# Two padding tensors wider by 128 bytes: where the low weights and the hidden activations begin in SBUF

## The reference

```
first block, layer 0:  x = ffn(x); z = ffn(z); x = conv(x); z = conv(z); x = ffn(x); z = ffn(z)
first block, layer 1:  x = ffn(x); z = ffn(z); x = attention(x, keys of x and z); x = ffn(x)
second block, 2 layers: x = x + 0.5*ffn(x); x = x + mix(x) @ w_out; x = x + 0.5*ffn(x)

ffn(h)  = (silu(h @ w_gate) * (h @ w_up)) @ w_down        # 1024 -> 2 x 2816 -> 1024
conv(h) = (b * shortconv(c * u)) @ w_out, with b, c, u = split(h @ w_in)   # 1024 -> 3 x 1024 -> 1024
```

## Time and profile before

| | us |
|---|---|
| three timed runs | 2809.34, 2808.19, 2803.70 |
| their median | 2808.19 |
| the profiled execution, its own time | 2811.81 |
| its span, first to last instruction | 2809.8 |
| PE busy in it | 2734.7 (97%) |
| DVE, ACT, POOL busy | 1814.3, 1340.4, 799.1 |

### The profile page before, as it was taken

One profiled execution on the slowest core, in us unless ns is written; L12 is line 12 of the kernel. 1 busy time (PEld: TensorE's weight loads), 2 busy tenths in 40 slices (PEclk: granted clock), 3 DMA queues, 4 the chain that ended last, 5 costly groups with the idle time before them and its releaser, 6 DMA issues.

```text
span 2809.8 us, 59491 instructions
## 1 busy us (share of the span) xinstructions
PE 2734.7 (97%) x23696; PEld 2622.2 (93%) x23696; DVE 1814.3 (65%) x2505; ACT 1340.4 (48%) x1872; POOL 799.1 (28%) x768
## 2 busy tenths in 40 slices
PE   6999999999999999999998999999999999999999
PEld 4999999999999999999986998999889999987999
DVE  4655746777648567466466765765876566488664
ACT  3434434455435344344345444445764454377543
POOL 1322412124314224034001330321743223046330
PEclk9999999999999999999999999999999999999999
DMA  8765666566666656666621454555325555541554
GB/s 310 260 250 208 241 244 209 207 235 226 237 227 227 231 203 240 224 227 240 231 70 61 158 189 147 186 196 189 128 81 196 195 177 192 193 157 64 182 193 148
DMA packets 151711, 546.43 MB, mean 194 GB/s; under 512 B 16688, under 2 KB 20576, under 8 KB 151136
## 3 DMA queue, kind: packets, MB, share of 16 engines
q1 hardware_dynamic: 147632, 534.84, 55.4%
q10 hardware_dynamic: 3888, 8.86, 0.9%
HBM read 541.80 MB, written 1.84 MB: 193 GB/s over the span
## 4 chain that ended last, share of the span: by engine, by line
PE 90%; DVE 6%; ACT 2%; issue 1%; DMA 1%; ACTq 1%; SPq 0%; DVEq 0%
PE ps L414 28%; PE ps L415 27%; PE ps L416 27%; PE ps L441 2%; DVE w_lo L394 1%; DMA modraw<-wmod 1%; PE ps L825 1%; PE ps L809 1%; PE ps L798 1%; ACTq L1562 0%; DVE xT L1956 0%; DVE h_lo L1606 0%; ACT w_hi L386 0%; PE ps L893 0%; PE ps L700 0%
## 5 line engine op out<-in xcount | busy, mean ns | idle before, releaser
L394 DVE TENSOR_TENSOR w_lo<-raw,w_hi 128x1024 fp32r<-128x1024 f32 x874 | 1128.5, 1308 | 627.7 <-ACT w_hi L386 626.2
L414 PE MATMUL ps<-h_hi,w_hi 128*128 128x256 f32 (+1 forms) x4928 | 1384.7, 281 | 25.8 <-DVE h_lo L1606 13.2
L415 PE MATMUL ps<-h_lo,w_hi 128*128 128x256 f32 (+1 forms) x4928 | 1367.6, 278 | 0.0
L416 PE MATMUL ps<-h_hi,w_lo 128*128 128x256 f32 (+1 forms) x4928 | 1366.6, 277 | 0.0
L386 ACT ACTIVATE w_hi<-raw 128x1024 fp32r<-128x1024 f32 x874 | 894.2, 1053 | 507.3 <-PE ps L416 501.3
L414 PEld LDWEIGHTS ps<-h_hi,w_hi 128*128 128x128 f32 x4928 | 928.7, 188 | 47.2 <-issue 27.4
L415 PEld LDWEIGHTS ps<-h_lo,w_hi 128*128 128x128 f32 x4928 | 930.4, 189 | 0.8
L416 PEld LDWEIGHTS ps<-h_hi,w_lo 128*128 128x128 f32 x4928 | 930.2, 189 | 0.0
L2270 POOL CAST u_hi<-ut 128x256 fp32r<-128x256 f32 (+1 forms) x258 | 246.8, 957 | 1307.1 <-DVE ut L1764 747.6
L415 PE MATMUL ps<-u_lo,w_hi 128*128 128x256 f32 (+1 forms) x2064 | 581.1, 282 | 0.0
L414 PE MATMUL ps<-u_hi,w_hi 128*128 128x256 f32 (+1 forms) x2064 | 580.1, 281 | 0.2 <-DVE ut L1658 0.2
(11 more groups left out here) (317 smaller groups left out, 1743.9 us busy)
## 6 DMA issues: line engine op xcount, KB each, us to landing
raw<-wst SPq DMA_DIRECT2D x874, 512.0 KB, 3.7
modraw<-wmod SPq DMA_DIRECT2D x132, 512.0 KB, 5.6
headraw<-wmod SPq DMA_DIRECT2D x12, 512.0 KB, 10.0
mtab<-mixtabs ACTq DMA_DIRECT2D x2, 1673.5 KB, 7.7
xT<-xin ACTq DMA_DIRECT2D x2, 1024.0 KB, 23.8
atab<-attabs ACTq DMA_DIRECT2D x1, 1024.0 KB, 6.3
out<-xT SPq DMA_DIRECT2D x1, 1024.0 KB, 4.8
skew<-sqb ACTq DMA_DIRECT2D x1, 768.0 KB, 3.3
```

The lines of the kernel that those rows point to most:

```text
L394: dve.tensor_tensor(w_lo[:, s, :], raw[:, s, :], w_hi[:, s, :], ALU.subtract).then_inc(S("lo_ready"), 1)
L414: pe.matmul(psum, wh, hi, start=start, stop=False)
L415: pe.matmul(psum, wh, lo, start=False, stop=False)
L416: return pe.matmul(psum, wl, hi, start=False, stop=stop)
```

## The change

The unused tensor `before_w_lo` grows from 16 to 48 floats a partition, 128 bytes more. Every tensor allocated after it starts 128 bytes later; no instruction, wait or transfer is different, and the order on every engine is the same.

```
         raw = sb("raw", [P, RING, D])
-        sb("before_w_lo", [P, 16])
+        sb("before_w_lo", [P, 48])
         w_lo = sb("w_lo", [P, RING, D], F32R)
```

## The result

| | before | after |
|---|---|---|
| median of the runs, us | 2806.60 | 2823.60 |
| lowest to highest (4 runs each) | 2803.70 to 2809.34 | 2820.97 to 2827.61 |
| span of the profiled execution, us | 2809.8 | 2825.6 |

The fourth run of the kernel before, beside the three listed ahead, took 2805.01 us. The ratio is 1.0058, 95% interval 1.0043 to 1.0073: the change made the kernel slower by 17 us, where 26.6 us less were forecast. One correction to the title: only one padding tensor, `before_w_lo`, grew. u moved because it is allocated behind it.

What follows compares the result with a forecast made beforehand. PE's pace through its own matmuls was taken to bound the kernel; 27.7 us gained on u less 1.1 given back, all else 0, took the median 2808.2 to 2781.6, given as 2782 us, range 2772 to 2808.

Steps and rivals of the forecast that it cites:

- PE is the path: Whole kernel: PE busy for 97% of the span, dense matmuls stepping at a fast 113.3 or slow 118.9 ns.
- u from 96 to 224: Stages on u: 206 of 258 slow units (24 matmuls each) turn fast, 134 ns each, saving 27.7 us.
- w_lo from 160 to 32: Low-weight load beside matmuls on h: h already runs at the fast pace and keeps it, 0 us.
- The upper bound that I gave for one slot: Matmuls on h at line 415: should they turn slow in all 4576 tiles, 25.6 us lost.
- 1.1 us given back at the first cout stage: First cout stage: its 1.1 us gain may only lengthen PE's wait for h's second half, so taken off.
- 258 columns: Stage with 258 columns on h, at 120.8 ns: 7.0 us gained or lost possible, 0 taken.
- D: Rival: the 258-column stage turns fast as well, 7 us more saved, 2775 us; chance 12%.
- The other tensors: Moved attention, mixing layer and norm tensors: at most some 6 us either way, 0 taken.
- C: Rival: w_lo at 32 slows h, at line 415 (25.6 us, about 2807) or all three slots (76.9 us, 2859); 11%.
- A: Rival: the pace belongs to how a run begins, not to the address; no change, 2808 us; chance 10%.
- B: Rival: only part of u turns fast, as places may count modulo 512; some 13 us saved, about 2795; 13%.

Runs made afterwards that it cites:

- the map: Not the full kernel: matmuls alone on PE, 48 in a row, over places of w_hi and w_lo; with 258 columns the 64 pairs took 117.7 to 124.3 ns.

## Why the prediction was wrong

- *PE is the path, and a step of the dense matmuls is 113.3 or about 118 ns.* Right; PE's busy time and the span moved together.
- *u from 96 to 224: 206 slow units, 27.7 us.* The size was right for that move alone: 26.3 us on u, 25 in the time of the kernel with u alone. The reason was wrong. The forecast gave it to the place of u; what counts is u's distance to w_hi and to w_lo at once, which the move of u without w_lo sets to those of h before.
- *w_lo from 160 to 32: "I take 0 for h".* This is the step that failed. I judged each matmul by its own pair: h beside w_hi at (224, 32) ran fast in two slots of three, so the third would too with w_lo at 32. The runs show that the three slots are one pattern. With w_hi at 64 and w_lo at 192 behind the moving operand every start ends in the fast pace; with w_lo at 64, where w_hi is, both paces hold and what ran before decides. It cost 24.2 us on h and left u mixed (13.4 us gained instead of 26.3). The upper bound that I gave for one slot, 25.6 us, is close to the cost by luck: it is all three slots, in about half of the stretches, each step slower by 4.5 ns and not 5.6.
- *1.1 us given back at the first cout stage.* Not shown: the wait behind the cout stages is 4.4 us in all, where it was 4.5, and it is 4.5 again in the kernel with u alone, where both cout stages are fast.
- *258 columns: 0.* Right within 0.8 us, and D falls with it; in the map no pair of places comes near the 114.2 ns that D asked for, the best being 117.7.
- *The other tensors: 0, within 6 us.* The span has some 6 us more than the dense steps explain; in the kernel with u alone some 4. That is inside the bound. By the same estimate 4.6 and 1.7 us of it (9.6 us in the trace of u alone, less the 7.9 of before) lie in the stretches at granted clock 0.50, a term that the forecast did not have; the cause of the remainder is open.
- *The rivals.* C named the place and the sign, at 11%. What spoke for it was in front of me in the earlier trace rows: one address of u with two paces says that the address alone is no cause, and that h might lose its single pace as easily as u might gain one. The forecast explained h's single pace by its own place, though its distances to w_hi and to w_lo differed from u's as well. A falls as an account of the whole, since the kernels with u alone have no slow stage of 256 columns; but at the other three pairs how a run begins does decide. B had the half of u that stays slow, but not its reason, which was modulo 512, and not the cost on h.

The Trainium skill, "SBUF — State Buffer", section "Who interferes with whom", lists PE's two read ports as independent and says that PE never waits on anyone. Taken as the forecast took it, that the start addresses cannot matter, this does not hold for the pattern: with PE alone at work the pace goes from 113.3 to 121.2 ns with the starts of the operands. That PE waits on another engine is not shown; the slow pace needs none.

## What to carry to other kernels

Where matmuls and their weight loads stream back to back, look at the pace from start to start, by operand and by stage; a group's mean duration hides it. If one tensor shows two paces, find what makes another tensor have only one, and copy all of its distances, not the one that comes to mind: for these matmuls w_hi at 64 and w_lo at 192 bytes behind the moving operand, modulo 256. Moving both "to be alike" removed the asymmetry that did the work; the best of these kernels moves u alone, 0.9909 of the time before.

## What the runs showed of the hardware

- The pace of back-to-back matmuls of 256 columns (type float32r, weights of 128 x 128) with weight loads beside them depends on where the operands start: 113.3 to 121.3 ns with nothing but PE at work. It repeats every 256 bytes. For starts at multiples of 32 bytes the one pair that is always fast goes by differences; 4 bytes off cost as much as a wrong pair, even where all operands are shifted alike.
- Some pairs have two stable paces at the same addresses. Which one a run takes depends on what PE did before it, and it can keep it for a whole stage (60 us and more), also through the branches of the loops.
- Why the fast pace needs 64 and 192 bytes, and in that order, these runs do not say.
